# Low parts of the weights: half of each unit made by GpSimd in the second mixer

## The reference

```python
# h = rmsnorm(x, mix_norm[i]);  z = h @ w_in[i]   (1024 -> 2560: q, k, v, memory q)
# kv = rmsnorm(mem, mem_norm[i]) @ w_mem_kv[i]
# q, k: norm over each head of 64, rotary; memory q, k: norm over each head
s = einsum('bqhcd,bkhcd->bhcqk', q_blk, k) * scale      # two score maps a head
p = softmax(where(allowed, s, NEG_INF))
a = p[:, :, 0] - lam * p[:, :, 1]                       # differential attention
y = norm over each head of 128 of (a @ v);  y_mem = softmax(q_m @ k_m) @ v_m
x = x + concat(y, y_mem) @ w_out[i]
```

## Time and profile before

| | |
|---|---|
| median of the runs | 1409.69 us |
| profiled execution, its own time | 1411.71 us |
| its span, first to last instruction | 1409.9 us |
| TensorE busy | 1380.1 us (98%) |
| VectorE busy | 939.5 us (67%) |
| ScalarE busy | 711.0 us (50%) |
| GpSimd busy | 128.1 us (9%) |
| the chain that ended last | TensorE 90%, VectorE 5%, ScalarE 2% |

### The profile page before, as it was taken

The page is one execution under the profiler, slowest core; times in us unless marked ns, Lnnn a source line. Parts: engine busy times, 40 slices in busy tenths (PEclk is TensorE's granted clock), DMA queues, the critical chain, the costliest instruction groups (busy, mean ns, idle before and its releaser), DMA issues.

```text
span 1409.9 us, 19718 instructions
## 1 busy us (share of the span) xinstructions
PE 1380.1 (98%) x7665; PEld 1183.8 (84%) x7665; DVE 939.5 (67%) x1158; ACT 711.0 (50%) x921; POOL 128.1 (9%) x145
## 2 busy tenths in 40 slices
PE   7999999999999999999999999999999989999998
PEld 5889998888888888888888888888888867788887
DVE  4975666766677666765567666666667778666665
ACT  4555445544464444577654444544445666554442
POOL 3000003000020000032020000100000321300000
PEclk9999999999999999999999999999999999999999
DMA  9454446755546555453355555465555532366551
GB/s 270 160 170 128 144 161 250 246 180 198 188 138 218 181 193 193 163 191 110 105 179 179 187 200 180 148 211 188 198 181 177 177 122 91 136 200 200 181 197 71
DMA packets 169549, 246.37 MB, mean 175 GB/s; under 512 B 5800, under 2 KB 130900, under 8 KB 169360
## 3 DMA queue, kind: packets, MB, share of 16 engines
q1 hardware_dynamic: 166048, 240.14, 51.0%
q0 software_dynamic: 1776, 4.74, 1.2%
q10 hardware_dynamic: 1664, 0.66, 0.2%
HBM read 244.45 MB, written 1.07 MB: 174 GB/s over the span
## 4 chain that ended last, share of the span: by engine, by line
PE 90%; DVE 5%; ACT 2%; issue 1%; DMA 1%; POOL 1%; SPq 0%; ACTq 0%; POOLq 0%; DVEq 0%
PE ps L1490 28%; PE ps L1442 15%; PE ps L1495 14%; PE ps L1443 14%; PE ps L1444 14%; PE ps L1731 2%; PE ps L1702 1%; DMA raw<-in_w_in 1%; ACT xx L547 1%; PE ps L1483 1%; DVE xx L892 1%; PE ps L1897 0%; ACT whi L512 0%; DVE wlo L846 0%; DVE wlo L1326 0%
## 5 line engine op out<-in xcount | busy, mean ns | idle before, releaser
L1490 PE MATMUL ps<-xx,whi 128*128 128x512 f32 x1760 | 443.6, 393 | 2.7 <-DVE xx L892 2.7
L1490 PEld LDWEIGHTS ps<-xx,whi 128*128 128x128 f32 x1760 | 318.7, 189 | 64.3 <-issue 3.6
L851 DVE TENSOR_TENSOR wlo<-raw,whi 128x2048 fp32r<-128x2048 f32 x120 | 275.1, 2293 | 94.0 <-ACT whi L520 94.0
L520 ACT ACTIVATE whi<-raw 128x2048 fp32r<-128x2048 f32 x120 | 229.5, 1913 | 122.5 <-PE ps L1444 122.5
L512 ACT ACTIVATE whi<-raw 128x2048 fp32r<-128x2048 f32 (+1 forms) x136 | 207.0, 1537 | 105.9 <-PE ps L1444 95.8
L1495 PEld LDWEIGHTS ps<-xx,wlo 128*128 128x128 f32 x1760 | 241.5, 190 | 18.1
L1495 PE MATMUL ps<-xx,wlo 128*128 128x256 f32 x1760 | 247.0, 283 | 0.0
L846 DVE TENSOR_TENSOR wlo<-raw,whi 128x2048 fp32r<-128x2048 f32 x76 | 173.3, 2288 | 34.8 <-ACT whi L512 34.7
L1442 PE MATMUL ps<-whi,hhi 128*128 128x512 f32 x488 | 193.5, 396 | 1.7 <-DVE hlo L1037 1.7
L1443 PE MATMUL ps<-wlo,hhi 128*128 128x512 f32 x488 | 191.3, 392 | 0.0
L1444 PE MATMUL ps<-whi,hlo 128*128 128x512 f32 x488 | 190.9, 391 | 0.0
(11 more groups left out here) (241 smaller groups left out, 1618.6 us busy)
## 6 DMA issues: line engine op xcount, KB each, us to landing
raw<-in_ffn_w_gate SPq DMA_DIRECT2D x44, 1024.0 KB, 5.1
raw<-in_ffn_w_up SPq DMA_DIRECT2D x44, 1024.0 KB, 5.2
raw<-in_ffn_w_down SPq DMA_DIRECT2D x44, 1024.0 KB, 4.8
raw<-in_w_in SPq DMA_DIRECT2D x41, 1024.0 KB, 5.1
raw<-in_w_gate_up SPq DMA_DIRECT2D x22, 1024.0 KB, 5.1
raw<-in_w_out SPq DMA_DIRECT2D x12, 1024.0 KB, 4.9
raw<-in_w_down SPq DMA_DIRECT2D x11, 1024.0 KB, 4.9
raw<-in_w_mem_kv SPq DMA_DIRECT2D x4, 1024.0 KB, 5.1
```

Source lines behind the costliest of these rows:

```text
L520: act.activation(whi[:, c % 3, :], raw[:, c % 3, :], ACT.Copy).then_inc(hi_done, 1)
L851: dve.tensor_tensor(wlo[:, c % 3, :], raw[:, c % 3, :], whi[:, c % 3, :], ALU.subtract)\
L1490: return pe.matmul(ps[:, bank + n, :], whi[:, slot, 256 * k + P * n:256 * k + P * n + P], both, start=start, stop=False)
```

## The change

In the second mixer (L = 1) VectorE makes only the first half of each unit's low part, and counts `lo_done` with it. GpSimd makes the second half of the fifteen units in `LO_POOL` (180 to 194) and counts it in a new semaphore, `lo_pool`. GpSimd's queue is now written by slots: a norm stands one slot after the slot in which its tile leaves TensorE, and the half of unit MEMU + (h+5)//4 at every fourth slot (h = 3, 7, ..., 59). Whoever waited for `lo_done` of such a unit waits for `lo_pool` too: SyncE before the buffer is filled again, TensorE before the unit's first matmul in `dense`, in `out_part`, ahead of `last_one` and ahead of the last feed-forward part. The first mixer stays as it is.

```diff
--- before.py
+++ after.py
@@ -101,6 +101,10 @@
 def tile_event(L, n):
 
     return n + (1 if L == 1 and n >= 8 else 0)
+
+
+
+LO_POOL = range(MEMU[1] + 2, FFU[4] + 1)
 
 
 def s_bank(i):
@@ -270,7 +274,7 @@
         memT_full, mem_hi, mem_lo, tile_ready = sem("memT_full"), sem("mem_hi"), sem("mem_lo"), sem("tile_ready")
         y_tr, y_hi, y_lo, sub_ready = sem("y_tr"), sem("y_hi"), sem("y_lo"), sem("sub_ready")
         out_full = sem("out_full")
-        hi_done, lo_done, unit_used = sem("hi_done"), sem("lo_done"), sem("unit_used")
+        hi_done, lo_done, lo_pool, unit_used = sem("hi_done"), sem("lo_done"), sem("lo_pool"), sem("unit_used")
         sq_done, rstd_ready, xn_ready, pool_ms = sem("sq_done"), sem("rstd_ready"), sem("xn_ready"), sem("pool_ms")
         tr_ps, xhi_done, xlo_done = sem("tr_ps"), sem("xhi_done"), sem("xlo_done")
         acc_ready, res_done = sem("acc_ready"), sem("res_done")
@@ -311,6 +315,8 @@
             def fill(u, slot, src, a):
                 if not isinstance(u, int) or u >= 3:
                     sp.wait_ge(lo_done, u - 2)
+                if isinstance(u, int) and u - 3 in LO_POOL:
+                    sp.wait_ge(lo_pool, u - 2 - LO_POOL[0])
                 sp.dma_start(raw[:, slot, :].rearrange("p (a b) -> p a b", a=a), src)\
                     .then_inc(raw_full[slot], 16)
 
@@ -485,17 +491,32 @@
                     row_scale(N_F3, 0.5)
                 norm(N_M0 + 3 * L)
                 e0 = E0[L]
-                for n in range(10):
+
+                def tile_norm(n):
                     e = e0 + tile_event(L, n)
-                    if n == 8 and L == 1:
-                        head_norm(e0 + SUB_EVENT[0], 4, 2 * HD)
                     if n in (4, 5):
                         query_norm(e, n - 4)
                     else:
                         head_norm(e, MH if n < 2 else 8, HD)
-                if L == 1:
-                    head_norm(e0 + SUB_EVENT[2], 4, 2 * HD)
-                    head_norm(e0 + SUB_EVENT[3], 4, 2 * HD)
+
+                def lo_half(c):
+                    pool.wait_ge(hi_done, c + 1)
+                    v = slice(1024, UW)
+                    pool.tensor_tensor(wlo[:, c % 3, v], raw[:, c % 3, v], whi[:, c % 3, v], ALU.subtract)\
+                        .then_inc(lo_pool, 1)
+
+                if L == 0:
+                    for n in range(10):
+                        tile_norm(n)
+                else:
+                    for h in range(SLOTS):
+                        if 0 <= h - 1 < 40 and (h - 1) % 8 in (5, 7):
+                            tile_norm(2 * ((h - 1) // 8) + ((h - 1) % 8 == 7))
+                        for g in (0, 2, 3):
+                            if h == V_AT[4 * g + 3] + 2:
+                                head_norm(e0 + SUB_EVENT[g], 4, 2 * HD)
+                        if h % 4 == 3:
+                            lo_half(MEMU[1] + (h + 5) // 4)
                 norm(N_F2 + 3 * L)
                 row_scale(N_F2 + 3 * L, 0.5)
 
@@ -1324,7 +1345,7 @@
                     dve.wait_ge(hi_done, c + 1)
                     v = slice(1024 * part, 1024 * part + 1024)
                     ins = dve.tensor_tensor(wlo[:, c % 3, v], raw[:, c % 3, v], whi[:, c % 3, v], ALU.subtract)
-                    if part:
+                    if part or c in LO_POOL:
                         ins.then_inc(lo_done, 1)
 
                 def heads_rest(h):
@@ -1418,7 +1439,7 @@
                         scores(i0 + S_AT.index(h))
                     if L == 1 and (h - 1) // 8 in (1, 3, 4) and (h - 1) % 8 in (5, 7):
                         rotated(2 * ((h - 1) // 8) + ((h - 1) % 8 == 7))
-                    if h >= 2 and (h + 6) % 4 < 2:
+                    if h >= 2 and (h + 6) % 4 < 2 - L:
                         lo_half(u + (h + 6) // 4, (h + 6) % 4)
                     if L == 1 and h in S_AT:
                         combine(i0 + S_AT.index(h))
@@ -1840,6 +1861,8 @@
                     c, n = u + 2 * s + half, 2 * s + r
                     if h % 4 == 0:
                         pe.wait_ge(lo_done, c + 1)
+                        if c in LO_POOL:
+                            pe.wait_ge(lo_pool, c + 1 - LO_POOL[0])
                     if h % 8 in (0, 2) and n >= 5:
                         pe.wait_ge(stream_evac, base + n - 2)
                     for k in (4 * half + 2 * kk, 4 * half + 2 * kk + 1):
@@ -1868,6 +1891,8 @@
                     m, r, c = (h - 48) // 4, h % 4 // 2, h % 2
                     if h % 4 == 0:
                         pe.wait_ge(lo_done, WO[1 + L] + m + 1)
+                        if L == 1:
+                            pe.wait_ge(lo_pool, WO[2] + m + 1 - LO_POOL[0])
                         pe.wait_ge(y_lo, 4 * L + m + 1)
                     if h in (48, 50):
                         pe.wait_ge(stream_evac, base + 11 + r)
@@ -1931,7 +1956,11 @@
                         turn_heads(h)
                     if h in Y_TURNS[L]:
                         turn_product(Y_TURNS[L][h])
+                if L == 1:
+                    pe.wait_ge(lo_pool, WO[2] + 4 - LO_POOL[0])
                 last_one(WO[1 + L] + 3, (4, 6), left(3), (y_lo, 4 * L + 4), T_F2 + 3 * L, R_WO1 + 3 * L)
+                if L == 1:
+                    pe.wait_ge(lo_pool, len(LO_POOL))
                 ffn(2 + 2 * L, FFU[2 + 2 * L], T_F2 + 3 * L, R_WO1 + 3 * L, T_F3 if L == 0 else None)
```

## The result

The changed kernel takes 1422.03 us (median of 4 runs, 1421.61 to 1423.75) against 1409.79 us (4 runs, 1408.27 to 1410.09): ratio 1.0089, 95% interval 1.0076 to 1.0101. It is slower by 12.2 us, far outside the range of 1406.0 to 1418.0.

The account below looks back on a forecast made before the run. VectorE was taken as full from 1140 to 1176 (busy 32.11 of 36.00 us), with at most 7.2 us of TensorE idle recoverable. Losses 5.2 less gain 2.25 gave about +3.0 on 1409.69, so 1412.7 us; range 1406.0 to 1418.0.

Parts of the forecast that it names:

- A VectorE instruction with two SBUF inputs waits for the whole of it: Upper bound taken for the operand port: such an instruction is held for GpSimd's entire subtraction, put at 2.1 us.
- The losses at the six places, 5.2 us: Holds of VectorE near 1120, 1131.5, 1151.30, 1167.2, 1172.38 and 1192.41: 0.6, 0.4, 1.2, 0.85, 1.5 and 0.65 us.
- The halving at 1120: Line 1355's scalings would be about 1.2 us late; requests lie 0.3 us apart, so half was counted: 0.6 us.
- The other eight meet idle time or instructions that read PSUM: GpSimd's subtractions outside the listed meeting places in the second mixer were claimed to cost VectorE nothing.
- The subtraction, 2.1 us: Length taken for each of GpSimd's fifteen new 128x1024 subtractions, between bounds of 0.98 and 2.8 us.
- The gain, 2.25 us: Removing fifteen VectorE half subtractions in the second mixer: 0.3 + 1.22 + 0.73 us.
- the three at 0.1: Near 1134.2, 1145.23 and 1186.5, the next VectorE instruction waits for ScalarE: at most 0.1 us gained each, 0.3 together.
- The "real" 1.22 at 1167.26: The next VectorE instruction's input was ready and VectorE ran without a gap, so removing the subtraction gains 1.22 us.
- Waits and queues at nothing: New TensorE and SyncE waits are answered early and refills land in time; TensorE's 0 to 0.5 us was taken as 0.
- VectorE is not held: Rival, chance 0.34: GpSimd asks for operands piece by piece and VectorE passes; -2.25 us, 1407.4 us.
- The chain is right: Rival, chance 0.14: each chain subtraction is worth its price, five times 1.2, up to 7.2 us idle; 1403.5 us.
- Longer subtraction, more meetings: Rival, chance 0.10: subtractions of 2.8 us, later ScalarE and a lower clock after stalls; +8.5 us, 1418.2 us.

Follow-up runs that it names:

- e3: Changed kernel with GpSimd's subtractions replaced by two fills that read nothing, second halves made by nobody; 1408.72 us, ratio 0.9993 to the kernel before.
- e1: Changed kernel with GpSimd subtracting only 8 columns of each second half, the rest made by nobody; 1408.61 us against 1409.83 for the kernel before.
- e6: Changed kernel with GpSimd making the second halves of units 180 to 192 only, VectorE the rest; 1418.45 us, ratio 1.0059 to the kernel before.
- e5: Changed kernel with GpSimd making the second halves of units 193 and 194 only, VectorE the rest; 1413.13 us, ratio 1.0027 to the kernel before.
- e11: The kernel before, unchanged, profiled a second time; own time 1410.03 us, mixer 124.46 us.
- e2: Changed kernel's order and waits, VectorE making both halves and waiting for 8 columns a unit from GpSimd; 1410.77 us, ratio 1.0010 to the kernel before.
- the first profile: The profile of the kernel before that the prediction was read from; own time 1411.71 us, mixer 127.55 us.

## Why the prediction was wrong

The mechanism was the right one. It failed because the list of places where GpSimd's subtraction holds VectorE was short, because the places on it and the clock cost more than was put down for them, and because half of the gain on the other side was not there.

e3 has VectorE's and GpSimd's instructions in the same order as the changed kernel, with fills for the subtractions, and its clock dips only once in the mixer: ahead of a wait of TensorE where the changed kernel's dips too and where it costs neither of them anything. So the lag of one behind the other can be read instruction by instruction: start in the changed kernel less 1089.25, minus start in e3 less 1089.01 (each mixer's first residual). In us:

```
held instruction            length (normal)  lag before -> once settled   predicted
1109.73 L1376               2.54 (0.43)       0.0 ->  0.1                 none
1117.78 L961, 1122.19 L1376 2.31, 3.24 for 2
                            (0.68, 1.28)      0.1 ->  1.9                 0.6
1134.80 L1021               1.43 (0.22)       1.9 ->  2.8                 0.4
1155.50 L993                1.62 (0.16)       2.8 ->  4.2                 1.2
1171.38 L993                1.03 (0.16)       4.2 ->  5.1                 0.85
1176.32 L1376               2.79 (0.68)       5.1 ->  6.3                 1.5
1188.47 L1347               2.00 (1.22)       6.3 ->  6.3                 none
1198.46 L1021               1.02 (0.22)       6.3 ->  7.1                 0.65
clock, 1203.5 to 1206.9                       7.1 ->  7.5                 none
1209.47 L1347               3.40 (1.22)       7.5 ->  9.7                 none
1216.48 L1404               2.85 (0.69)       9.7 -> 11.7                 none
clock, 1220.6 to 1224.0                      11.7 -> 13.3                 none
```

13.3 us is also the distance of the medians (1422.03 and 1408.72). Read against e1, the hold at 1155.50 seems to cost nothing, and the total is 11.9. That is e1's own clock: its dip comes just behind the wait and makes e1 itself 1.4 us later there. The same place in the changed kernel, e3 and e1:

```profile
1158.41 0.39 PE L1463 MATMUL ps<-heads_t 64*128 64x256 f32 x2 [1.57 <-ACT pr L597]
...
1153.95 0.39 PE L1471 MATMUL ps<-heads_t 64*128 64x256 f32 x2
...
1152.76 0.39 PE L1467 MATMUL ps<-heads_t 64*128 64x256 f32 x2 [1.69 <-ACT pr L601]
...
1154.51 0.63 PE L1468 MATMUL ps<-wlo,xx 128*128 128x512 f32 x1
```

e6, whose clock does not dip near this place, has the same lag behind e3 on both sides of the hold, 2.8 and 4.2.

Point by point:

- **"A VectorE instruction with two SBUF inputs waits for the whole of it": right.** This bound was chosen against the one in which GpSimd yields. The eleven lengths show it, and e3 shows that it is the reading. (The Trainium skill, "SBUF — State Buffer", "Who interferes with whom", calls the shared pair an exclusive lock and says that a VectorE instruction with two SBUF inputs contends with a GpSimd instruction that reads SBUF. That whoever issues first has the pair for the whole instruction, it says of VectorE's two-port modes; the prediction took it for this case too. The runs agree, 0.69 us becoming 2.85 beside 2.36, and also with the restriction to GpSimd instructions that read SBUF: 0.69 stays 0.69 beside the fill.)
- **The losses at the six places, 5.2 us: they cost 7.0** (1.8, 0.9, 1.4, 0.9, 1.2, 0.8; the first holds the uncounted meeting at 1117.78 too, which can't be told apart from it). The halving at 1120 and "met at its edge" near 1131 were hopes. At 1122.19 the subtraction had started 0.3 us ahead and at 1134.80 1.0 us, and VectorE was held by 1.96 and 1.21.
- **"The other eight meet idle time or instructions that read PSUM": this step failed.** (Six and eight are fourteen, of fifteen subtractions.) Five more held a two-input instruction. Those at 1109 and 1188 cost 0.1 and nothing. The last two cost 4.2 us and lie on the path. I checked the places against the old VectorE timeline and not against what GpSimd's new order releases: the subtraction stands right behind the norm for which VectorE's scaling waits, so scaling and subtraction start together. At 1209.47 it is VectorE's own half, released by the same high part as GpSimd's. e5 shows the pair alone: 3.3 us.
- **The clock, 2.0 us, was only in a rival.** TensorE stands still for 1.88 us at 1219.38 and works at the lower level from 1220.57. A stall is not always answered so: in e5 no dip follows the same stall. So that the stalls bring the dips is not shown; what is shown is that these two cost the changed kernel 2.0 us in this profile.
- **The subtraction, 2.1 us: measured 2.36 to 2.41**, between the bounds 0.98 and 2.8. At eleven meetings the 0.3 us are at most 3 us. (The estimate of 2.25 us from the Trainium skill, "GPSIMD Engine Reference", section 3, was nearer.)
- **The gain, 2.25 us: measured 1.1 to 1.2.** (By e3 the medians say 1.1, with zero just inside the interval; the mixers of e11 and e3 say 1.25, 124.46 and 123.21.) Of its terms the three at 0.1 were rightly small: `1150.60 0.16 DVE L1020 RECIPROCAL` now waits `[1.16 <-ACT pr L597]`. The "real" 1.22 at 1167.26 gave 0.3. VectorE is earlier by 1.13 us in e3 than in e11, and gives it back 7 us later, waiting for TensorE:

```profile
1172.97 0.69 DVE L1402 TENSOR_TENSOR xn<-ps,rec 128x512 f32<-128x512 f32 x1
1174.68 0.29 DVE L1014 CUSTOM_DVE_ANT_0 sc<-ps,cst 128x128 f32<-128x128 f32 x1 [1.02 <-PE ps L1473]
```

  I had followed VectorE to 1174 and called the stretch gapless, but the scores that it turns to next come from TensorE's queue, which was not ahead. The term of the last sub-norm, 0.73, was 1.0.
- **Waits and queues at nothing: right** within e2's +0.9. (TensorE gets 15 new waits, not 18.)

From the forecast of +3.0 to the measured 12.2: the two missed places 4.2, the clock 2.0, the counted places 1.8, the smaller gain 1.1 and the 0.1 at 1109 add 9.2 us, and the account closes. It is read from single profiles, so each term is good to a few tenths.

Profiles also differ ahead of the mixer. It starts at 1087.8 us in the first profile, e1 and e2 and at 1088.9 or later in the others. Between the first profile and e11 the whole difference is there by 35 us (VectorE's subtraction at 33.67 and 35.05) and stays the same for the next 1054 us. In those first 30 us 7 of the first profile's 128x512 matmuls and 19 of e11's are longer than 0.55 us. So this too is the clock and not the change.

The rival "VectorE is not held" is refuted, "The chain is right" by e1 and e3 (its price, 1403.5, is neither five times 1.2, which gives 1403.7, nor the 7.2 us of idle, which give 1402.5). "Longer subtraction, more meetings", with a chance of 0.10, came nearest: more meetings and the clock were true, the 2.8 us were not, and its +8.5 was short.

## What to carry to other kernels

Before work is moved from VectorE to GpSimd, list every GpSimd instruction that will read SBUF and every two-input VectorE instruction near it, in the new order: above all those that one GpSimd instruction or one event releases together, since these always meet. Work that GpSimd must do is cheaper in short instructions; work that is only in VectorE's way is better moved in VectorE's own order. And a gain is real only when the instruction after the next wait for another engine is earlier too.

## What was not expected of the hardware

- The hold does not depend on the size of the held instruction: a product of two elements per partition (line 993, 0.16 us) waited 1.46 us.
- At the last sub-norm the scaling of 0.69 us became 1.22, 1.50, 1.76 and 2.85 us beside GpSimd instructions of 0.74 (the median of the 128x256), 1.04, 1.28 and 2.36 us that began 0.06 to 0.08 us earlier. The stretch is what is left of the GpSimd instruction, less 0.13 to 0.15 us.
- A GpSimd instruction with one SBUF input holds VectorE as one with two does.
- Two profiles of one kernel differ by 3.1 us in a mixer of 125 (127.55 and 124.46), and all of it is the clock. Half a dozen 128x512 matmuls at 0.63 us instead of 0.40, with the transposes between them, cost 1.4 us behind a wait of TensorE and nothing ahead of it.
